# Six norms of a two-model kernel computed in two halves of the tokens, three decay levels merged into one, one exponential moved ahead of copies

## The chip, the cores and the metric

The kernel runs on one core of one Trainium2 chip. The metric is the device time of one execution in microseconds (us); the median of a few runs is compared with that of the kernel before. A profiled execution gives the trace that is read here.

## The reference, cut to what matters

Two transformer stacks run one after the other on a residual stream x of 256 tokens by 1,024 channels, all in fp32.

The first stack has two layers. Each takes h = rms_norm(x) * (1 + sc1) + sh1, multiplies it by `w_in`, runs three mixers on the parts (A: axial rotary attention; B: a gated linear recurrence in both directions of time; C: dilated local attention), and adds g1 * (mix @ `w_out`) to x. A second norm, a gated convolutional feed-forward (`w_up`, `w_down`) and a second addition follow. Mixer B needs attn[t, s] = sum over k of q[t,k] * key[s,k] * exp(b[t,k] - b[s,k]) for s <= t, b being the running sum of the logarithm of the forget gate, and the mirror of it backwards.

The second stack has a "fox" attention layer and an "NSA" attention layer, each followed by a norm and by experts (PEER): 8 heads choose 16 of 16,384 experts for each token. The factors sc, sh and g are 1,024-long dot products of a condition vector with the rows of "ada" matrices.

Every norm needs a mean over all channels of x, so it needs all output tiles of the product before it.

## The kernel before

**Layout.** Channels lie on the 128 partitions and tokens along the free dimension: `xT` and `hT` are [128, 8, 256]. A product is made tile by tile: `tile_T` (L748) takes one 128x1024 block of weights (a unit, 512 KB) from `ring`, a ring of eight, and accumulates eight fp32 matmuls of 256 columns into half of one PSUM bank. Each fp32 matmul is two MATMUL and two LDWEIGHTS instructions in the trace. Two tiles are a job in one of four banks (`open_job` L736, the plan L513 to L547).

**A norm** (`norm_stat` L741, `norm` of ScalarE L1183 and of VectorE L1651, `residual` L1659). There are eight, o = 0 to 7. VectorE adds job k of the product before into `xT` (L1666), ScalarE squares two channel tiles (L1188), TensorE sums all squares by eight matmuls with ones, ScalarE takes the root (L1190), VectorE the reciprocal (L1649), then scales the eight channel tiles (L1656), ScalarE shifts each (L1195), and the next product begins at the first shifted tile. Norms 1 and 3 stand between `w_out` and `w_up` of the two layers, 2 and 4 after `w_down`, 5 and 7 after the output products of the second stack and before the expert queries ("pq"); 0 is the first, and 6 stands between the experts and NSA.

**Decay levels** (mixer B; `level` L774, `decay` L1207, the loop L1802). The decay is not factored over a whole sequence but by halving blocks. Level k has blocks of 256 >> k tokens and takes the reference of b in the middle of each, so that no exponent is positive. VectorE forms the differences (L1808), ScalarE two pairs of exponentials (L1219), VectorE multiplies keys and queries with them (L1816, L1817), TensorE makes eight matmuls of 128 columns, and VectorE copies what is new under a mask (L1828). There are eight levels and a ninth without decay, the diagonal. Levels 0 to 5 stand between tiles of `w_in`; 6, 7 and the diagonal come after the last of them. Rotary steps of mixer A (L1790 to L1798) stand beside steps 6 and 7 on VectorE. Attention begins when all nine are copied (L867).

**Queues.** SP issues the units and the ada loads in an order written out by hand (L662 to L701). An ada load has one of four slots and waits for VectorE's dot product of four before (L645); `do_ada` (L1622) on VectorE waits for the load. In layer 0, 20 ada loads stand between units 27 and 28, and tiles 6 and 7 of `w_out` are made of units 28 and 29. In the fox layer two ada loads follow each unit from the eighth on (L701), 16 in all; VectorE makes their dot products (L2083) ahead of the forget-gate steps (L2089 to L2097), for which ScalarE waits (L1474) ahead of further copies.

**Experts** (L929, L1258, L1982). VectorE picks experts (`choose` L1906); the first choice's gates need ScalarE's exponential (L1328) of a difference that VectorE makes at L1934. ScalarE comes to it behind two copies of tokens (L1278) and six transfers that it issues itself (L1282). TensorE turns the first choice (`rows_of` L972) after the fourth expert unit of the first group.

## Time and profile before

| | us |
|---|---|
| median of 3 runs (2563.29 to 2564.15) | 2563.31 |
| profiled execution | 2559.09 |
| its span, first to last instruction | 2557.3 |
| TensorE matmul busy | 2438.8 |
| weight loads busy | 2276.6 |
| VectorE busy | 1630.7 |
| ScalarE busy | 849.5 |
| GpSimd busy | 282.0 |

The profiled execution lies 4.2 us under the median. Matmuls overlap, so TensorE's busy time is read as the time in which something was in the array. The mean granted TensorE clock is 0.983 of full speed. DMA moved 729 MB at 285 GB/s on average.

### The profile page before, as it was taken

Reading aid. Unit: us, or ns where it says so; the run is one execution under the profiler, and the core shown is the slowest. Engines: PE = TensorE matmul, PEld = TensorE weight load, DVE = VectorE, ACT = ScalarE, POOL = GpSimd, SP = SyncE. Lnnn points to the kernel's source line nnn. Section 1 sums busy time; section 2 is a strip of 40 time slices with the busy share of each in tenths; the row PEclk is TensorE's granted clock in tenths of the full one; section 3 lists DMA queues with packets and bytes.
Section 4 is the critical chain, followed back from the end, with each engine's and each line's share of the span. In section 5 each row is a group of like instructions: output and inputs, shape, how many; then the busy total and the mean of one; then the engine's idle time right before and its main releaser. Section 6 shows DMA issues by size and latency. Waiting matters only on the chain.

```text
span 2557.3 us, 44536 instructions
## 1 busy us (share of the span) xinstructions
PE 2438.8 (95%) x16628; PEld 2276.6 (89%) x16628; DVE 1630.7 (64%) x3720; ACT 849.5 (33%) x2165; POOL 282.0 (11%) x374
## 2 busy tenths in 40 slices
PE   5978999989999999999999999999999999999999
PEld 4867888878888888899999999988888999999999
DVE  6685664575565562497788884333637958888733
ACT  2541110254211022222665551012532246655300
POOL 0020110001011001011111111100210101111111
PEclk8999999999999999999999999999999999999999
DMA  9327887521687873399999999964026999999997
GB/s 365 117 81 262 302 308 286 198 84 43 246 305 271 312 266 98 114 370 414 342 403 385 404 406 412 397 243 164 18 83 227 404 355 401 408 379 410 408 414 297
DMA packets 172059, 729.13 MB, mean 285 GB/s; under 512 B 19216, under 2 KB 19728, under 8 KB 146960
## 3 DMA queue, kind: packets, MB, share of 16 engines
q1 hardware_dynamic: 143568, 523.92, 55.2%
q0 software_dynamic: 27648, 201.34, 19.4%
q10 hardware_dynamic: 704, 2.10, 0.3%
q8 instruction: 77, 1.26, 0.2%
q14 instruction: 62, 0.51, 0.1%
HBM read 724.14 MB, written 1.05 MB: 284 GB/s over the span
## 4 chain that ended last, share of the span: by engine, by line
PE 87%; DVE 5%; DMA 3%; ACT 3%; issue 2%; ACTq 0%; SPq 0%; DVEq 0%
PE banks L721 39%; PE lev L1019 22%; PE banks L965 20%; PE lev L721 2%; DMA extra<-in_ada 1%; DMA ring<-in_peer_u 1%; PE lev L946 1%; PE banks L946 1%; ACT arena L1219 1%; DVE arena L1632 1%; DVE arena L1776 1%; DVE rstd L1649 1%; ACT arena L1245 1%; DMA arena<-in_ada 0%; PE lev L818 0%
## 5 line engine op out<-in xcount | busy, mean ns | idle before, releaser
L721 PE MATMUL banks<-hT,ring 128*128 128x256 f32 x2832 | 631.3, 386 | 41.8 <-ACT hT L1195 40.9
L721 PEld LDWEIGHTS banks<-hT,ring 128*128 128x128 f32 x2832 | 547.6, 194 | 124.0 <-issue 45.3
L965 PE MATMUL banks<-hT,ring 128*128 128x160 f32 x4096 | 578.8, 301 | 2.3 <-DMA ring<-in_peer_u 2.3
L1019 PE MATMUL lev<-arena,ring 128*128 x4096 | 576.5, 301 | 0.0
L965 PEld LDWEIGHTS banks<-hT,ring 128*128 128x128 f32 x4096 | 559.2, 190 | 3.4 <-DMA ring<-in_peer_u 2.0
L1019 PEld LDWEIGHTS lev<-arena,ring 128*128 128x128 f32 x4096 | 558.9, 190 | 0.0
L1603 POOL DMA_INDIRECT arena<-in_peer_rows,keysb x192 | 184.2, 959 | 1147.7 <-DVE consts L1992 671.3
L721 PE MATMUL banks<-arena,ring 128*128 128x256 f32 (+1 forms) x1344 | 280.6, 371 | 6.0 <-DMA ring<-in_stream_first 4.6
L721 PEld LDWEIGHTS banks<-arena,ring 128*128 128x128 f32 x1344 | 246.4, 191 | 38.7 <-issue 5.0
L2039 DVE SCALAR_TENSOR_TENSOR extra<-consts,chT 128x192 bf16<-128x192 f32 x640 | 223.7, 409 | 26.5 <-ACT arena L1286 26.4
L2004 DVE CUSTOM_DVE_ANT_0 arena<-arena 128x1024 f32<-128x1024 f32 x64 | 78.2, 1222 | 166.0 <-DMA arena<-in_peer_rows,keysb 166.0
L1632 DVE CUSTOM_DVE_ANT_0 arena<-arena 128x1024 f32<-128x1024 f32 x104 | 127.6, 1227 | 58.8 <-DMA arena<-in_ada 55.4
L1992 DVE SCALAR_TENSOR_TENSOR consts<-arena,extra,consts 128x1024 f32<-128x1024 f32 x128 | 164.0, 1281 | 0.0
L2004 DVE CUSTOM_DVE_ANT_0 arena<-arena,consts 128x1024 f32<-128x1024 f32 x128 | 155.5, 1215 | 0.3
L1286 ACT ACTIVATE arena<-banks 128x320 f32<-128x320 f32 x128 | 55.8, 437 | 275.1 <-PE banks L965 256.8
L1580 POOL TENSOR_SCALAR arena<-arena,rinv 128x256 f32<-128x256 f32 (+1 forms) x128 | 63.4, 508 | 729.0 <-DVE rinv L1703 557.6
L1311 ACT ACTIVATE std<-consts,chT 128x128 bf16<-128x128 f32 x320 | 102.1, 390 | 82.7 <-PE banks L946 65.9
L1632 DVE CUSTOM_DVE_ANT_0 arena<-extra,arena 128x1024 f32<-128x1024 f32 x88 | 109.2, 1240 | 31.6 <-DMA extra<-in_ada 28.2
L1311 ACT ACTIVATE rstd<-consts,chT 128x128 bf16<-128x128 f32 x320 | 102.0, 390 | 73.3 <-PE banks L946 54.6
L1436 ACT ACTIVATE arena<-banks,params 128x256 f32<-128x256 f32 x88 | 44.9, 561 | 244.6 <-PE banks L721 244.6
L1300 ACT ACTIVATE extra<-extra 128x1 f32<-128x1 f32 x192 | 37.3, 194 | 265.5 <-DVE extra L2004 265.5
L721 PE MATMUL lev<-arena 128*128 128x128 f32 (+1 forms) x544 | 101.6, 331 | 23.3 <-DVE arena L1817 16.1
(275 smaller groups left out, 2254.3 us busy)
## 6 DMA issues: line engine op xcount, KB each, us to landing
ring<-in_peer_u SPq DMA_DIRECT2D x256, 512.0 KB
ring<-in_peer_v SPq DMA_DIRECT2D x256, 512.0 KB
ring<-in_stream_first SPq DMA_DIRECT2D x192, 512.0 KB
arena<-in_ada SPq DMA_DIRECT2D x104, 512.0 KB, 5.2
extra<-in_ada SPq DMA_DIRECT2D x88, 512.0 KB, 5.3
ring<-in_stream_nsa SPq DMA_DIRECT2D x45, 512.0 KB
ring<-in_stream_fox SPq DMA_DIRECT2D x41, 512.0 KB
arena<-in_peer_rows,keysb POOLq DMA_INDIRECT x192
```

What stands on the lines that cost most here:

```text
L721: ins = nc.tensor.matmul(o, lhsT, rhs, start=start, stop=stop, **kw)
L946: ins = nc.tensor.matmul(gate_banks[half][k % 2][:, t * 256:t * 256 + HALF], hot_r[:, k % 2, t], hot_c[:, k % 2, t, i], start=i == 0, stop ...
L965: ins = nc.tensor.matmul(banks[k // 2 % 4][:, (k % 2) * ND:(k % 2 + 1) * ND], ring[:, u % RING, c], hT[:, c, NS:T], start=c == 0, stop=c = ...
L1019: ins = nc.tensor.matmul(lev[c // 4][:, (c % 4) * T + NS:(c % 4 + 1) * T], ring[:, u % RING, c], a[:, bass.ds(g, 1), k], start=False, stop ...
L1286: A(acts_g[:, g, 2 * k:2 * k + 2], banks[k][:, 0:2 * ND].rearrange("p (a t) -> p a t", a=2), ACT.Gelu_apprx_tanh).then_inc(sem("act_freed" ...
L1311: A(dist[q % 2][:, t], iota, ACT.Abs, bias=chT[:, 0, 4 * q + t:4 * q + t + 1])\
L1580: G.tensor_scalar(x, x, rinv[:, u % 4, hh:hh + 1], 1.0, ALU.mult, ALU.mult).then_inc(sem("probs_ready"), 1)
L1603: G.indirect_dma_start(out=rows[:, n % ROWS], out_offset=None, in_=io["peer_rows"], in_offset=bass.IndirectOffsetOnAxis(ap=eid[:, k:k + 1] ...
L1632: seq(V.tensor_tensor_reduce(out=junk, in0=ada_slot(n), in1=crow[:, l // DEPTH], scale=1.0, scalar=0.0, op0=ALU.mult, op1=ALU.add, accum_o ...
L1992: V.scalar_tensor_tensor(out=y, in0=rows[:, n % ROWS, D:2 * D], scalar=row_act[:, k:k + 1], in1=y, op0=ALU.mult, op1=ALU.add).then_inc(sem ...
L2004: V.tensor_tensor_reduce(out=u, in0=u, in1=xn[i], scale=1.0, scalar=0.0, op0=ALU.mult, op1=ALU.add, accum_out=row_act[:, k:k + 1]).then_in ...
L2039: ins = V.scalar_tensor_tensor(out=hot_c[:, q % 2, t], in0=iota[:, half * HALF:(half + 1) * HALF].unsqueeze(1).broadcast_to([P, PARTS, HALF]),
```

## The change

Three edits. (1) In norms 1, 2, 3, 4, 5 and 7, the last two output tiles are made for tokens 0 to 127 first and 128 to 255 after, each half in its own bank; the addition, the squares, the sum, the root, the reciprocal, the scaling and the shift are done by half, and the first two tiles of the next product too. The two units of such a pair are waited for together and released together. VectorE's ada turns are moved off the fourth job (`ADA_OUT` 4, 4, 3, 3 to 5, 5, 4, 0; turns of 6 to 8, 8, 8, 0), and `mods` stand before the addition of the first half. (2) Decay levels 5, 6 and 7 become one, with blocks of eight tokens and the reference in their middle; its exponents may be positive. Its product is made twice, from the 64 partitions of each direction of time, and copied under two masks; the diagonal comes before these two. (3) In the experts the first exponential stands ahead of ScalarE's token copies; the turning of the choices and ScalarE's part of it stand two units later.

```diff
+NDEC, NLEV = 6, 8
...
+    lv[:, 8], lv[:, 9] = np.where(fwd, 1, -1), np.where(fwd, -1, 1)
...
+    same = [(p[:, None] // b == p[None] // b) for b in (64, 32, 16, 8)]
+    lm = same[:3] + [np.eye(P), same[3] & (p[:, None] < p[None]), same[3] & (p[:, None] > p[None])]
...
+        def plan_halves(o):
+            for t in range(TT):
+                plan(("half", o), 1, t)
+                plan(("norm", o), 1, t)
...
             plan(("up", l), FC)
-            plan(("down", l), 4)
-        plan(("norm", 4), 1)
+            plan(("down", l), 3)
+            plan_halves(2 * l + 2)
...
-        ADA_TURNS = [[24] + [2] * FC + [6] * 4, [0] + [2] * FC + [6] * 4]
...
+        ADA_TURNS = [[24] + [2] * FC + [8, 8, 8, 0], [0] + [2] * FC + [8, 8, 8, 0]]
+        ADA_LEVELS, ADA_UNITS, ADA_OUT = [4, 0], [[0] * 6 + [1] * 6, [0] * NATT], [(5, 5, 4, 0), (0, 0, 0, 0)]
...
-                    state["pending"] = True
+                    state["pending"] -= 1
+
+            def next_unit(hold=False):
+
+                if hold:
+                    state["held"] += 1
+                elif state["unit"] >= 0:
+                    state["pending"] += 1 + state["held"]
+                    state["held"] = 0
                 state["unit"] += 1
...
+            def norm_part(o, t, chunks):
+
+                b = open_job("norm", o, t) if 0 in chunks else bank_of("norm", o, t)
+                for c in chunks:
+                    if t == 0 and c == 6:
+                        pe.wait_ge(sem("sq_half"), HALVED.index(o) + 1)
+                    elif c % 2 == 0:
+                        pe.wait_ge(sem("sq_ready"), 4 * o + c // 2 + 1)
+                    mm(b[:, 0:P], ones, sq[:, c, half_of(t)], c == 0, c == DC - 1,
+                       None if c < DC - 1 else filled("norm", o, t)[0])
+
...
+
+                w = [next_unit(), next_unit(hold=True)]
+                for t in range(TT):
+                    b = open_job("half", o, t)
+                    for k in range(2):
+                        for c in range(DC):
+                            mm(b[:, k * P:(k + 1) * P], w[k][:, c], src[:, c, half_of(t)], c == 0, c == DC - 1,
+                               filled("half", o, t)[0] if k and c == DC - 1 else None)
+                        if t and not k:
+                            norm_part(o, 0, (6, 7))
+                    norm_part(o, t, range(6))
+
+            def first_tiles(j, o):
...
+
+                n = HALVED.index(o)
+                b = open_job(*j)
+                w = [next_unit(), next_unit(hold=True)]
+                for t in range(TT):
+                    for k in range(2):
+                        for c in range(DC):
+                            if k == 0:
+                                pe.wait_ge(*((sem("h_ready"), DC * o + c + 1) if t else (sem("h_half"), DC * n + c + 1)))
+                            mm(b[:, k * T + t * P:k * T + (t + 1) * P], w[k][:, c], hT[:, c, half_of(t)], c == 0, c == DC - 1,
+                               filled(*j)[0] if t and k and c == DC - 1 else None)
+                        if t == 0 and k == 0:
+                            norm_part(o, 1, (6, 7))
 
...
                     pe.wait_ge(sem("lev_freed"), g - 1)
                 if l > 0 and k < 2:
...
-                qq = eq[:, k % 2] if k < 8 else qB
+                at = min(k, NDEC - 1)
+                if k != 5:
+                    pe.wait_ge(sem("keys_decayed"), l * NDEC + at + 1)
+                    pe.wait_ge(sem("queries_decayed"), l * NDEC + at + 1)
+                kk, qq = (fk, qB) if k == 5 else (ek[:, at % 2], eq[:, at % 2])
+                side = slice(0, HD) if k == 6 else slice(HD, P) if k == 7 else slice(0, P)
                 out_ = lev[g % 2][:, :].rearrange("p (h t q) -> p h t q", h=4, t=TT)
                 for h in range(4):
                     for t in range(TT):
...
                            signal=sem("lev_filled") if h == 3 and t == 1 else None)
...
                            signal=sem("lev_filled") if h == 3 and t == 1 else None)
 
...
+                for k in (6, 7):
                     level(l, k)
-                pe.wait_ge(sem("lev_freed"), 9 * (l + 1))
+                pe.wait_ge(sem("lev_freed"), NLEV * (l + 1))
...
-                for k in range(4):
...
-                norm_stat(2 * l + 1)
-                for k in range(FC):
+                last_tiles(2 * l + 1, mixT)
...
 
+                o = 2 * l + 2
+                halves = [open_job("half", o, t) for t in range(TT)]
+                for c in range(FC):
+                    at = 6 * FC + c
+                    if at % 8 == 0:
+                        w = next_unit()
+                    for t in range(TT):
+                        mm(halves[t][:, 0:P], w[:, at % 8], zT[:, c, half_of(t)], c == 0, c == FC - 1)
+                blocks = []
+                for t in range(TT):
+                    for c in range(FC):
+                        at = 7 * FC + c
+                        if t == 0:
+                            if at % 8 == 0:
+                                w = next_unit(hold=True)
+                            blocks.append(w[:, at % 8])
+                        mm(halves[t][:, P:2 * P], blocks[c], zT[:, c, half_of(t)], c == 0, c == FC - 1,
+                           filled("half", o, t)[0] if c == FC - 1 else None)
+                        if t and c == 7:
+                            norm_part(o, 0, (6, 7))
+                    norm_part(o, t, range(6))
...
-                inputs(NG // 2 - 1, NG // 2, False, {2: turn_choices})
+                inputs(NG // 2 - 1, NG // 2, False, {4: turn_choices})
...
+
...
+                n = HALVED.index(o)
+                for k in range(3):
+                    wait(sem("x_ready"), 4 * (o - 1) + k + 1)
+                    square(k, full, "sq_ready")
+                wait(*freed("half", o, 0))
+                square(3, half_of(0), "sq_half")
+                root(0, half_of(0))
+                for c in range(DC):
+                    wait(sem("half_scaled"), 8 * n + c + 1)
+                    shift(c, half_of(0), "h_half")
+                    if c == 1:
+                        wait(sem("x_ready"), 4 * (o - 1) + 4)
+                        square(3, half_of(1), "sq_ready")
+                root(1, half_of(1))
                 for c in range(DC):
...
             def drain(dst, *j):
...
+                    wait(sem("lev_filled"), l * NLEV + k - 1)
+                if k == NDEC - 1:
+                    for dst, c in ((eq, 8), (ek, 9)):
+                        A(dst[:, k % 2], dl[:, k % 2], ACT.Exp, scale=lvl[:, c:c + 1]).then_inc(sem("decays"), 2)
+                    return
                 d = dl[:, k % 2].rearrange("p h (n s m) -> p (h n) s m", s=2, m=m)
...
+
+                exp_of(0, 0)
                 wait(sem("xn_filled"), p + 1)
...
-                exp_of(0, 0)
...
                         choices()
                 for step in range(2 * GATES):
...
 
...
+                    add(bank_of("half", o, t), 3, half_of(t), P, freed("half", o, t))
+
+                def scale(t, c, signal):
...
-                        else:
-                            ins.then_inc(sem("x_half"), 1)
-                    wait(*freed(*name, k))
+                    add(bank_of(*name, k), k, slice(0, T), T, freed(*name, k))
                     dve.sem_inc(sem("x_ready"), 1)
+                do_ada(beside[3])
+                if late:
+                    late()
+                add_half(0)
+                wait(*freed("norm", o, 0))
+                seq(V.reciprocal(rstd[:, half_of(0)], std[:, half_of(0)]))
+                for c in range(DC):
+                    scale(0, c, "half_scaled")
+                    if c == 1:
+                        add_half(1)
+                        dve.sem_inc(sem("x_ready"), 1)
+                wait(*freed("norm", o, 1))
+                seq(V.reciprocal(rstd[:, half_of(1)], std[:, half_of(1)]))
+                for c in range(DC):
+                    scale(1, c, "h_scaled")
 
...
 
             def k_norms(dst, raw, rs, lo, hi):
...
```

## Rows read from the trace of the kernel before

**Rows 1.** the page, part 1 and the first two lines of part 5 for TensorE.
```profile
PE 2438.8 (95%) x16628; PEld 2276.6 (89%) x16628; DVE 1630.7 (64%) x3720; ACT 849.5 (33%) x2165; POOL 282.0 (11%) x374
...
L721 PE MATMUL banks<-hT,ring 128*128 128x256 f32 x2832 | 631.3, 386 | 41.8 <-ACT hT L1195 40.9
L721 PEld LDWEIGHTS banks<-hT,ring 128*128 128x128 f32 x2832 | 547.6, 194 | 124.0 <-issue 45.3
```

**Rows 2.** waits of TensorE: engine, line, waited for: us in total, times, longest.
```profile
PE banks L721 <- ACT hT L1195: 40.9, 8, 15.9
...
PE lev L721 <- DVE arena L1817: 16.1, 6, 4.4
...
PE banks L721 <- DMA ring<-in_stream_first: 4.6, 1, 4.6
PE lev L1044 <- DVE arena L1965: 4.6, 2, 2.7
```

**Rows 3.** timeline around norm 3: start, us, engine, line, operation, count [idle before <-releaser].
```profile
648.94 0.63 ACT L1188 ACTIVATE arena<-xT 128x512 f32<-128x512 f32 x1 [6.27 <-DVEq L1674]
651.42 0.47 ACT L1190 ACTIVATE std<-banks,epsc 128x256 f32<-128x256 f32 x1 [1.85 <-PE banks L721]
651.93 1.75 DVE L1649 RECIPROCAL rstd<-std 128x256 f32<-128x256 f32 x1 [3.08 <-ACT std L1190]
653.72 3.26 DVE L1656 SCALAR_TENSOR_TENSOR hT<-xT,gscale,rstd 128x256 f32<-128x256 f32 x8
654.24 3.31 ACT L1195 ACTIVATE hT<-hT,mod 128x256 f32<-128x256 f32 x8 [2.34 <-DVE hT L1656]
...
654.89 9.48 PE L721 MATMUL banks<-hT,ring 128*128 128x256 f32 x35 [3.51 <-ACT hT L1195]
```

**Rows 4.** stretches: A:B us, PE, PEld, DVE, ACT, POOL busy (count), PEclk, DMA.
```profile
652.74:656.15 3.41, 1.26 (x6) 1.16 (x7) 3.37 (x8) 1.91 (x5) 0.00 (x0) 1.00 0.00 0
656.15:659.56 3.41, 3.41 (x10) 2.66 (x9) 0.82 (x3) 1.39 (x4) 0.00 (x0) 0.50 0.48 154
567.40:581.06 13.66, 9.31 (x42) 9.07 (x43) 10.31 (x12) 1.92 (x3) 0.00 (x0) 0.50 0.00 1
```

**Rows 5.** chain that ended last: start, us, what.
```profile
83.10 6.91 PE banks L721 x32
...
102.20 7.16 PE banks L721 x64
...
209.33 6.66 DMA ring<-in_stream_first
...
920.54 6.29 DMA extra<-in_ada
```

**Rows 6.** ScalarE instructions of 128 columns, by form.
```profile
L1311 ACT ACTIVATE std<-consts,chT 128x128 bf16<-128x128 f32 x320 | 102.1, 390 | 82.7 <-PE banks L946 65.9 <-PE lev L946 16.3
```

**Rows 7.** timeline of TensorE, output tiles 6 and 7 of layer 0.
```profile
216.12 8.69 PE L721 MATMUL banks<-arena,ring 128*128 128x256 f32 x32 [4.63 <-DMA ring<-in_stream_first]
```

**Rows 8.** timeline of TensorE, statistics of fox queries and keys.
```profile
936.48 1.12 PE L721 MATMUL banks<-arena,consts 128*128 128x512 f32 x2 [2.00 <-ACT arena L1465]
```

**Rows 9.** timeline of layer 0 from the sixth level to the attention.
```profile
127.61 1.23 DVE L1816 TENSOR_TENSOR arena<-arena 128x1024 f32<-128x1024 f32 x1 [9.57 <-ACT arena L1219]
...
130.00 1.30 DVE L1828 COPY_PREDICATED arena<-arena,lev 128x1024 f32<-128x1024 uint32 x1
...
131.66 6.20 ACT L1219 ACTIVATE arena<-arena,consts 128x512 f32<-128x512 f32 x8
...
137.34 3.64 PE L721 MATMUL lev<-arena 128*128 128x128 f32 x16 [4.42 <-DVE arena L1817]
...
138.57 0.69 DVE L1790 TENSOR_TENSOR arena<-banks,consts 128x512 f32<-128x512 f32 x1
...
150.92 1.99 PE L721 MATMUL lev<-arena 128*128 128x256 f32 x8 [1.45 <-DVE arena L1828]
```

**Rows 10.** timeline of the first experts' choice: token copies, exponential, TensorE's wait.
```profile
1085.10 3.48 ACTq L1282 DMA_DIRECT2D arena<-extra  x4
...
1090.26 0.22 DVE L1959 TENSOR_REDUCE gsum<-arena 128x4 f32<-128x64 f32 x1 [6.08 <-ACT arena L1292]
...
1093.31 0.61 PE L1044 MATMUL lev<-arena,consts 128*64 128x96 f32 x12 [1.87 <-DVE arena L1965]
```

More of the change, by code:

```diff
@@ L525, in build @@
         plan(("attF",), 8)
-        plan(("foxout",), 4)
-        plan(("norm", 5), 1)
+        plan(("foxout",), 3)
+        plan_halves(5)
         for k in range(4):
@@ L717, in _ @@
         def _(pe):
-            state = {"unit": -1, "pending": False}
+            state = {"unit": -1, "pending": 0, "held": 0}
             def mm(o, lhsT, rhs, start=True, stop=True, signal=None, **kw):
@@ L1069, in _ @@
             mixed[0] = [(sem("conv_out"), 1)]
-            for k in range(4):
+            for k in range(3):
                 b = open_job("foxout", k)
@@ L1165, in _ @@
             mixed = {c: [freed("attN", 2 * c + t) for t in range(TT)] for c in range(8)}
-            for k in range(4):
+            for k in range(3):
                 b = open_job("nsaout", k)
@@ L1192, in norm, with square, root @@
-                l, w = o // 2, o % 2
+                l, w = o // 2, o % 2
+                def square(k, of, signal):
+                    A(sq[:, 2 * k:2 * k + 2, of], xT[:, 2 * k:2 * k + 2, of], ACT.Square).then_inc(sem(signal), 1)
+                def root(t, of):
+                    wait(*filled("norm", o, t))
+                    b = bank_of("norm", o, t)
+                    A(std[:, of], b[:, 0:of.stop - of.start], ACT.Sqrt, bias=epsc[:, :], scale=1.0 / D)\
+                        .then_inc(freed("norm", o, t)[0], 1)
@@ new lines, in shift @@
+                def shift(c, of, signal):
+                    A(hT[:, c, of], hT[:, c, of], ACT.Identity, bias=mod[:, l, 3 * w, c:c + 1]).then_inc(sem(signal), 1)
+                full = slice(0, T)
+                if o not in HALVED:
+                    for k in range(4):
+                        if o:
+                            wait(sem("x_ready"), 4 * (o - 1) + k + 1)
+                        square(k, full, "sq_ready")
+                    root(0, full)
+                    for c in range(DC):
+                        wait(sem("h_scaled"), 8 * o + c + 1)
+                        shift(c, full, "h_ready")
+                    return
@@ new lines, in norm @@
+                n = HALVED.index(o)
+                for k in range(3):
+                    wait(sem("x_ready"), 4 * (o - 1) + k + 1)
+                    square(k, full, "sq_ready")
+                wait(*freed("half", o, 0))
[7 more added lines that the diff above has]
+                        square(3, half_of(1), "sq_ready")
@@ L1657, in norm, with residual, add, add_half @@
                                            op0=ALU.mult, op1=ALU.mult).then_inc(sem("h_scaled"), 1)
-            def residual(name, l, which, beside=(0, 0, 0, 0)):
-                for k in range(4):
+            def residual(o, name, l, which, beside=(0, 0, 0, 0), late=None):
+                def add(b, k, of, w, signal):
+                    for j in range(2):
+                        c = 2 * k + j
+                        V.scalar_tensor_tensor(out=xT[:, c, of], in0=b[:, j * w:(j + 1) * w],
+                                               scalar=mod[:, l, which, c:c + 1], in1=xT[:, c, of],
+                                               op0=ALU.mult, op1=ALU.add).then_inc(signal[0] if j else sem("x_half"), 1)
+                    wait(*signal)
+                def add_half(t):
+                    wait(*filled("half", o, t))
+                    add(bank_of("half", o, t), 3, half_of(t), P, freed("half", o, t))
+                def scale(t, c, signal):
+                    V.scalar_tensor_tensor(out=hT[:, c, half_of(t)], in0=xT[:, c, half_of(t)],
+                                           scalar=gscale[:, o // 2, o % 2, c:c + 1], in1=rstd[:, half_of(t)],
+                                           op0=ALU.mult, op1=ALU.mult).then_inc(sem(signal), 1)
+                for k in range(3):
```

135 lines of the change are left out of this document (56 added, 79 removed).

## The prediction

> **What bounds the kernel.** The engine line of the page comes first: TensorE is busy for 2438.8 us of 2557.3 [rows 1], so the kernel is a stream of matmuls with some 118 us of gaps, and a change is worth what it takes out of the gaps, less what it adds to the stream. The waits of TensorE say where the gaps are [rows 2]. For the first shifted tile of a norm: 40.9 us in eight waits, 15.9 of them at the kernel's start, so 3.57 for each of the other seven. For the decay levels: 16.1 in six. For the first expert choice: 4.6 in two. For a unit of weights: once, 4.6. The timeline of one norm shows a gap as a chain [rows 3]: root 0.47, reciprocal 1.75, one scaling, one shift, hand-overs; 3.51 idle. The stretches add its second price [rows 4]: with TensorE idle for most of 652.74 to 656.15, the next 3.41 us are granted half the clock (1.2 instead of 2.4 GHz), which costs half of them, 1.7. The other norm gaps are followed by the same, and in the levels of layer 1 the half clock lasts 13.66 us.
>
> **Narrow matmuls.** 64 of 128 columns take 7.16, 32 of 256 take 6.91 [rows 5]: 0.112 against 0.216, so two halves cost 0.008 more than a whole. Norms 1, 3, 5 and 7 turn 80 wide instructions into 160 (+0.64 each), 2 and 4 with their 22-deep products 136 into 272 (+1.1): 4.7 us in all. The Trainium skill (TensorE: Matmul & The Clock Gate, Back-to-back issue gap) speaks against this: in a stream of weight loads and matmuls it gives 81 ns at 128 columns where a lone one has 56, since the load sets the pace too. By that the 1184 narrow instructions would cost an estimated 30 us instead of 4.7.
>
> **A norm in halves, on one clock.** Time 0 is where TensorE, done with the first half of the last pair, begins six of its eight sums (1.34). Slopes for narrow operations: ScalarE 0.39 for 128 columns [rows 6], spaced about 0.30, root 0.37; VectorE takes 1.23 for 1024 and 0.69 for 512 columns [rows 9], so 1.05 ns a column: a scaling 0.35, spaced 0.26; the reciprocal 0.95 (half of 1.75 and some fixed cost). Additions of half 0 end at 0.9, squares at 1.35. TensorE has 1.34 of sums and 1.79 of second-half tile before it needs them at 3.13: no wait. Last sums at 3.58, root at 4.15, reciprocal 5.20, first shifts at 6.0 and 6.3; TensorE has the other tile (1.79) and six sums (1.34) until 6.71: no wait for chunks 0 and 1. VectorE then adds half 1, so chunk 2 comes at 7.45 and the rest 0.30 apart against 0.22 for a tile: the tile ends at 9.16 instead of 8.50, stall 0.66. Last sums of half 1 at 9.61; one tile (1.79) covers a chain of 2.58, stall 0.79; its eight shifts are spaced 0.30, stall 0.51. Sum 1.96, in three parts with matmuls between them; none is near the 3.51 after which the clock fell, and I take no loss of clock. Against it stand 3.72 (gap, and the first matmul's start) and 1.68 of clock: gain 3.72 + 1.68 - 1.96 - 0.64 = 2.8. After `w_down` it is 2.4.
>
> **The norms one by one.** 3, 5 and 7: 8.4. 2: 2.4. 1: unit 28 lands 6.66 us after its issue, behind 20 ada loads [rows 5], and TensorE waits 4.63 for it [rows 7]. The pair now starts when unit 29 has landed too, an estimated 1.25 later (729 MB in 2557 us is 1.8 us a unit on average, and the queue is fuller here); turns 5, 5, 4 let SP issue unit 28 when it did before, since the tenth dot product is bound by its load. 2.8 less 1.0 is 1.8. 4: the fox layer has 16 ada loads behind unit releases, then dot products, the forget gate, ScalarE's copies, and TensorE waits 2.00 for these [rows 8]; the last load takes 6.29 [rows 5] in a chain of four such rounds. Its third load follows unit 8, and unit 8 follows the release of unit 0, now held until the first pair is done: from the same start about 0.5 to 1.2 later than now. TensorE arrives 2.5 earlier and waits that much more. No gain, -0.8, and with some 5 us idle a lost clock stretch, taken at 1.4: -2.2. Norms together: 10.4.
>
> **Levels.** Before, after the sixth level (ended 132.9) TensorE waits 4.42 and again for levels 6 and 7, and attention starts at 150.92 [rows 9]. After: the merged decay is two exponentials of 1024 columns, 1.9 us in place of four at 2.9, both before level 5's place, so multiplications (2 x 1.2) end at 129.0; copy of level 4 1.3, rotary 3 x 0.7, copy of the diagonal from 133.0 to 134.3, rotary and key halves 2.9, then two copies of 1.3 end at 139.9. TensorE makes the two products by 136.5 and waits 3.4. Attention at 140.0: 10.9 earlier. Removed are VectorE's two differences and four multiplications, one copy, eight exponentials (6.20 [rows 9]), one product. Layer 1 has the same waits and twice the half clock [rows 4]: 12.0. The idle 3.4 may still cost a stretch of clock at the start of attention, mostly hidden by VectorE's work there; 0.6 each. Levels: 21.7.
>
> **Exponential.** VectorE waits 6.08 for it, because ScalarE issues transfers of 0.6 to 1.1 us each first; then 3.0 us of VectorE work end at 1093.3, where TensorE has waited 1.87 [rows 10]; the other layer makes it 4.6 [rows 2]. Moved, it ends at 1083.1 (a table load of 1.28), the choice at 1087.2, 4 us before TensorE wants it. The copies start 0.3 later; their transfers are first used by VectorE's rows, 30 us on. Row fetches begin some 5 us earlier and share the DMA with units; TensorE waits little there and I take 0. The choices turned two units later leave ScalarE 9 us for 5 us of work. Gain 4.6.
>
> **Sum.** 10.4 + 21.7 + 4.6 = 36.7. The profiled execution's 2559.1 becomes 2522.4. It lies 4.2 under the median 2563.3, which becomes 2526.6, my forecast. Alone it has 2516 to 2537.
>
> **Rivals.** (a) The halves give nothing: the scaling and shift chain waits for its own hand-overs twice, stalls double to 4, and the clock falls in some. For: three stalls instead of one, ScalarE waits 2.34 for a first scaling even now. Against: each is covered by 1.8 to 3.1 of matmuls. 36.7 - 10.4: 2537, up to 2543 with a lost stretch in each. 0.14. (b) Attention starts with the levels but its own chain (a reciprocal of 1.75 ahead of each of the first steps, outputs of mixer B at half clock) returns 10 of the 21.7: 2537. Against: that chain starts with the last copy in both kernels. 0.08. (c) The moved exponential does not do what it says, because VectorE next waits for the chosen rows or fetches take the DMA: 2531. 0.04. (d) Narrow matmuls stand 25 ns further apart, as in the page's rule: 1184 of them, 2551. The row of 64 in 7.16 is against it. 0.02. (e) Slower: a narrow matmul with new weights takes as long as its weight load, 0.194 [rows 1]. 1184 x (0.194 - 0.108) = 102 in place of 4.7: 2623. It turns slower where the spacing passes 0.143. Against: the same 0.112. 0.03. More than forecast, below 2516: 0.02. The forecast has 0.67.
>
> The range reaches from 2514 (all bounds on the good side: norm 4 even, no lost clock in attention, and 2 us of waits for DMA gone) to 2543, the end of (a). What a measurement of this kernel can tell from no change is about 0.2%, 5 us. Only (e) is slower; the same needs (a), (b) and (c) together.
>
> **What would show it.** Right: waits for L1195's successor fall from 3.5 to under 2.1 us in all for each halved norm, with clock 1.00 after them; the stretch from the sixth level to attention falls from 18 to 7 us; no wait of `rows_of`; the wait for fox statistics grows from 2.0 to about 5; tiles 6 and 7 of layer 0 start about 1 us later than now. Wrong: halved-norm waits above 3 us, narrow matmuls spaced over 0.12, or attention that starts early and ends no earlier.

## The result and the profile after

The changed kernel takes 2523.18 us (median of 4 runs, 2521.95 to 2524.96) beside 2563.30 of the kernel before (4 runs, 2560.57 to 2564.15): ratio 0.9846, 95% interval 0.9829 to 0.9863, so 40.1 us faster, where 36.7 were forecast. Run again later it took 2523.76 beside 2561.10, ratio 0.985 (0.9836 to 0.9863). The profiled execution has a span of 2523.2 after 2557.3: 34.1 less. It was the slowest of its four, while the profiled one of before lay 4.2 under its median, so 6 us of the gain don't show in the two traces. How much of the time TensorE's clock takes differs from execution to execution, and that is the main lesson of this case.

The page of the changed kernel, parts 1 and 5, answers to [rows 1]:

```profile
PE 2434.6 (96%) x17188; PEld 2288.6 (91%) x17188; DVE 1624.6 (64%) x3772; ACT 848.0 (34%) x2205; POOL 281.4 (11%) x374
...
L732 PE MATMUL banks<-hT,ring 128*128 128x256 f32 (+1 forms) x3024 | 631.9, 370 | 22.6 <-ACT hT L1279 22.4
L732 PEld LDWEIGHTS banks<-hT,ring 128*128 128x128 f32 x3024 | 554.0, 192 | 97.5 <-issue 21.7
```

TensorE issues 560 instructions more and is busy for 4.2 us less. It was busy at half clock for 64.0 us in the trace of before and for 40.0 in this one, which is worth 12.0 us of busy time; that outweighs what the narrow matmuls add. The other 29.9 of the 34.1 us are idle time that is gone. The waits of TensorE answer to [rows 2]:

```profile
PE banks L732 <- ACT hT L1279: 22.4, 8, 15.7
PE banks L732 <- ACT arena L1270: 18.7, 4, 14.7
...
PE lev L732 <- DVE arena L1968: 7.1, 2, 3.6
PE banks L732 <- issue: 4.2, 1, 4.2
PE banks L732 <- DVE arena L2223: 3.0, 1, 3.0
PE banks L1047 <- DMA ring<-in_peer_u: 3.0, 7, 0.8
PE banks L732 <- ACT arena L1581: 2.0, 1, 2.0
...
PE lev L732 <- DVE arena L1957: 1.2, 2, 0.6
```

One more line of the kernel before belongs beside these, the waits for copied levels:

```profile
PE lev L721 <- DVE arena L1828: 2.9, 2, 1.4
```

Waits for shifted tiles fell from 40.9 to 22.4, of which 15.7 is the start and 3.8 norm 6, still whole, which leaves 0.48 for each of the six halved norms. The levels cost 8.3 in four waits (7.1 for copies, L1968, and 1.2 for decayed queries, L1957), where before it was 19.0 in eight (2.9 for copies, L1828, and 16.1 for decayed queries, L1817). The wait at `rows_of` is gone. Two lines are new or larger: the statistics of fox (L2223 and L1581, 5.0 together, 2.00 and 0.88 before), and the small waits for units in the experts (3.0 in seven, 2.3 in three before).

Norm 3 in halves, in the timeline of the changed kernel (start, us, engine, line, operation, count [idle before <-releaser]), answers to [rows 3]:

```profile
620.37 1.95 PE L732 MATMUL banks<-arena,ring 128*128 128x128 f32 x16
...
622.80 0.37 ACT L1275 ACTIVATE std<-banks,epsc 128x128 f32<-128x128 f32 x1 [2.51 <-PE banks L732]
623.28 0.95 DVE L1804 RECIPROCAL rstd<-std 128x128 f32<-128x128 f32 x1 [3.44 <-ACT std L1275]
...
624.65 0.69 ACT L1279 ACTIVATE hT<-hT,mod 128x128 f32<-128x128 f32 x2 [1.48 <-DVE hT L1790]
...
625.73 2.62 PE L732 MATMUL banks<-hT,ring 128*128 128x128 f32 x16
...
630.60 2.45 ACT L1279 ACTIVATE hT<-hT,mod 128x128 f32<-128x128 f32 x8 [1.40 <-DVE hT L1790]
...
631.05 5.19 PE L732 MATMUL banks<-hT,ring 128*128 128x128 f32 x36 [0.48 <-ACT hT L1279]
```

And its stretches (A:B us, busy of PE, PEld, DVE, ACT, POOL with counts, PEclk, DMA share, GB/s), which answer to [rows 4]; the last four are the start of attention in the two layers:

```profile
631.05:635.21 4.16, 4.16 (x32) 4.16 (x33) 1.36 (x6) 2.00 (x7) 0.00 (x0) 1.00 0.44 174
635.21:642.10 6.89, 6.89 (x34) 6.09 (x33) 4.40 (x8) 1.02 (x2) 0.00 (x0) 1.00 0.75 271
137.55:140.96 3.41, 0.94 (x2) 0.84 (x3) 3.34 (x3) 0.00 (x0) 0.00 (x0) 0.50 0.00 0
140.96:144.38 3.42, 3.42 (x11) 2.81 (x10) 2.94 (x3) 1.02 (x4) 0.00 (x0) 0.50 0.02 5
553.97:557.39 3.42, 1.09 (x3) 0.92 (x4) 3.35 (x3) 0.00 (x0) 0.00 (x0) 0.50 0.00 0
557.39:560.80 3.41, 3.41 (x12) 2.87 (x11) 2.94 (x3) 1.02 (x4) 0.00 (x0) 0.50 0.00 0
```

Three small stalls stand where one of 3.51 was: sixteen instructions take 2.62 with shifts in step against 1.95 without (0.67), then 0.48 idle, then 32 in 4.16 where 32 at 0.112 take 3.57 (0.59). Together 1.74, and the clock is 1.00 behind them.

**Where the 34.1 us of the two traces come from.** The same point of the stream is looked up in both traces (start of a group of matmuls on the timeline), and the lead of the changed kernel is the difference.

| point | before | after | lead | gained since |
|---|---|---|---|---|
| w_out of layer 0 | 193.09 | 183.84 | 9.25 | levels 9.25 |
| second pair of w_up, layer 0 | 240.50 | 227.57 | 12.93 | norm 1: 3.68 |
| first level of layer 1 | 512.53 | 497.40 | 15.13 | norm 2: 2.20 |
| w_out of layer 1 | 622.63 | 597.23 | 25.40 | levels 10.27 |
| second pair of w_up, layer 1 | 663.56 | 635.21 | 28.35 | norm 3: 2.95 |
| second pair of fox | 900.38 | 871.68 | 28.70 | norm 4: 0.35 |
| first gap of fox attention | 988.53 | 964.29 | 24.24 | fox statistics: -4.46 |
| token copies' transposes | 1081.70 | 1054.51 | 27.19 | norm 5: 2.95 |
| second half of the experts | 1385.08 | 1355.44 | 29.64 | exponential: 2.45 |
| NSA attention, last gap | 1868.99 | 1838.32 | 30.67 | 1.03, clock behind norm 6 |
| transposes of the last experts | 1945.24 | 1911.62 | 33.62 | norm 7: 2.95 |
| second half of the last experts | 2248.41 | 2214.28 | 34.13 | exponential: 0.51 |

These are one execution of each kernel. Where the other traces tell more, the text below gives their numbers.

### The profile page after: what moved, and what is told of

Read it like the earlier page. It is cut to its first block, busy times and chain, and to the rows that moved or that the text cites. A ratio compares the mean times of both kernels' runs of the same rounds, so it can differ in the third digit from the quotient of the medians.

```text
span 2523.2 us, 45753 instructions
## 1 busy us (share of the span) xinstructions
PE 2434.6 (96%) x17188; PEld 2288.6 (91%) x17188; DVE 1624.6 (64%) x3772; ACT 848.0 (34%) x2205; POOL 281.4 (11%) x374
## 4 chain that ended last, share of the span: by engine, by line
PE 84%; DMA 7%; DVE 5%; ACT 2%; issue 2%; SPq 0%; DVEq 0%; ACTq 0%
PE banks L732 36%; PE lev L1101 22%; PE banks L1047 20%; DMA ring<-in_peer_u 3%; DMA extra<-in_ada 3%; PE lev L732 2%; DMA arena<-in_ada 1%; DVE arena L1748 1%; PE lev L1028 1%; PE banks L1028 1%; ACT arena L1361 0%; ACT arena L1335 0%; PE lev L873 0%; DVE arena L1832 0%; DVE arena L1968 0%
## 5 line engine op out<-in xcount | busy, mean ns | idle before, releaser
L732 PE MATMUL banks<-hT,ring 128*128 128x256 f32 (+1 forms) x3024 | 631.9, 370 | 22.6 <-ACT hT L1279 22.4
L732 PEld LDWEIGHTS banks<-hT,ring 128*128 128x128 f32 x3024 | 554.0, 192 | 97.5 <-issue 21.7
L732 PE MATMUL banks<-arena,ring 128*128 128x256 f32 (+2 forms) x1648 | 284.7, 334 | 5.5 <-issue 4.2
L732 PEld LDWEIGHTS banks<-arena,ring 128*128 128x128 f32 x1648 | 258.7, 192 | 30.3 <-issue 4.6
L1748 DVE CUSTOM_DVE_ANT_0 arena<-extra,arena 128x1024 f32<-128x1024 f32 x88 | 109.2, 1241 | 22.4 <-DMA extra<-in_ada 19.6
L1995 DVE SCALAR_TENSOR_TENSOR arena<-banks,params,arena 128x255 f32<-128x255 f32 x88 | 42.5, 483 | 107.4 <-ACT arena L1552 105.8
```

Source lines behind the costliest of these rows:

```text
L732: ins = nc.tensor.matmul(o, lhsT, rhs, start=start, stop=stop, **kw)
L1748: seq(V.tensor_tensor_reduce(out=junk, in0=ada_slot(n), in1=crow[:, l // DEPTH], scale=1.0, scalar=0.0, op0=ALU.mult, op1=ALU.add, accum_o ...
```

## The experiments

Twelve runs, each timed beside the kernel before. The times of before, in three groups of runs, were 2564.91, 2561.10 and 2561.82 (medians), so ratios are compared across groups. Each interval is about 0.0014 (3.6 us) to either side.

### The parts alone

Merged levels alone: on the kernel before, every hunk of the diff that has `NDEC`, `NLEV`, the masks or `decay` in it.

```
+NDEC, NLEV = 6, 8
...
-                for k in (6, 7, 8):
+                for k in (6, 7):
                     level(l, k)
```

> The kernel before with the merged decay levels alone. By the prediction's sum: 21.7 us off, so 2563.3 becomes 2541.6. By the marks of the two traces (start of attention, and the last attention gap, in each layer) it gives 9.25 in layer 0 and 10.25 in layer 1, 19.5, so 2543.8: 1.65 of each layer's gain is lost again in the first 3.4 us of attention, which run at half clock. Rival (b), that attention's own chain returns ten: 2552.

Measured: 2542.83, ratio 0.992 (0.9906 to 0.9934), 22.1 us between medians. The prediction's 21.7 stands; rival (b) falls.

The exponential alone, on the kernel before:

```
+                exp_of(0, 0)
                 wait(sem("xn_filled"), p + 1)
...
-                exp_of(0, 0)
                 done = 0
...
-                    if n == 28:
+                    if n == 29:
...
-                inputs(NG // 2 - 1, NG // 2, False, {2: turn_choices})
+                inputs(NG // 2 - 1, NG // 2, False, {4: turn_choices})
```

> The kernel before with the early exponential and the choices turned two units later alone. By the prediction: 4.6 us off (1.87 and 2.69 of waits at the first choice), 2558.7. By the traces, part of it comes back later in the experts as waits for units of weights, because the fetched rows start earlier and share the DMA: 3.1 off, 2560.2, with waits for units of more than 2 us in the profile. Rival (c), nothing comes of it: 2563.

Measured: 2556.24 (8 runs), ratio 0.9972 (0.996 to 0.9984): 8.7 us between medians, and 4.1 to 10.3 by the interval of the ratio, which still holds the prediction's 4.6 but not the 3.1. Rival (c), that nothing comes of it, falls.

Levels and exponential, both edits together, norms whole:

> The changed kernel with all norms whole: levels and exponential only. If the parts add, it stands 10.4 us above the changed kernel by the prediction, 10.6 by the marks of the traces: 2533.8 beside 2523.2. If halving gives nothing (rival a), it stands at the changed kernel's time, 2523. If halving interacts with the rest, it stands elsewhere than the sum of its parts run alone.

Measured: 2540.81, ratio 0.9915 (0.9899 to 0.993). The changed kernel stands 17.0 us lower (2523.76 in the next group), by the ratios 0.0065 or 16.7. The two intervals together leave 11 to 22 us for this difference. Trace against trace it is 12.9 and 13.7. Rival (a) falls, and halving is worth more than the 10.4 of the prediction, by how much is not certain.

### What a whole norm costs

The kernel of levels and exponential with the gap of each of the six norms filled by work that nothing reads:

```
 def norm_stat(o):
...
+    if o in (1, 2, 3, 4, 5, 7):
+        b = open_job("fill", o, 0)
+        for c in range(DC):
+            mm(b[:, 0:T], ones, cos, c == 0, c == DC - 1,
+               filled("fill", o, 0)[0] if c == DC - 2 else freed("fill", o, 0)[0] if c == DC - 1 else None)
```

> Levels and exponential only, all norms whole (as run third, 2540.8), with sixteen instructions of 128x256 on constants, 3.45 us, in the gap of each of the six norms that the change halves. It tells the two parts of a whole norm's price apart. Theory: the gap stays (now filled), and the half clock behind it goes; over five profiles with whole norms TensorE was busy at half clock for 22.7 us on average behind the six gaps, half of which is lost, so 11 us off, 2529 to 2530, and halving was worth 6 us of gaps besides. If the stretches of half clock do not come from the gaps: 2541.

Measured: 2527.81, ratio 0.9871 (0.9854 to 0.9888): 13.0 us under the kernel with whole norms (0.0044, 11.3, by the ratios), though no chain is shorter and TensorE runs 96 instructions more. The timeline of norm 1, first without and then with the filling:

```profile
214.60 3.62 PE L724 MATMUL banks<-arena,consts 128*128 128x256 f32 x16
221.79 8.51 PE L724 MATMUL banks<-hT,ring 128*128 128x256 f32 x25 [3.57 <-ACT hT L1199]
```

```profile
214.84 3.62 PE L730 MATMUL banks<-arena,consts 128*128 128x256 f32 x16
218.29 3.62 PE L730 MATMUL banks<-consts 128*128 128x256 f32 x16
222.03 3.26 PE L730 MATMUL banks<-hT,ring 128*128 128x256 f32 x14
```

Without it, the sum and the first tile lie 3.57 apart, and 25 instructions take 8.51. With it, the tile starts no sooner, and 14 take 3.26, the full rate. The stretches behind them, without and with:

```profile
220.80:224.21 3.41, 2.42 (x6) 2.00 (x7) 3.08 (x8) 3.07 (x8) 0.00 (x0) 0.50 0.04 7
224.20:227.60 3.40, 3.40 (x10) 2.68 (x9) 0.00 (x0) 0.24 (x1) 0.00 (x0) 0.50 0.42 152
```

```profile
222.00:226.00 4.00, 3.97 (x19) 3.53 (x20) 2.11 (x6) 2.68 (x7) 0.00 (x0) 1.00 0.41 135
```

So most of what halving won was the half clock behind the gaps, 11 to 13 us for six. What is left between this kernel and the changed one, 4 us by medians and 5 by the ratios, is what the gaps themselves won, less what fox gives back. Norm 3 shows both parts without mixture, from the start of `w_out` to the second pair of `w_up`, layer 1: 40.93 us in the three traces in which one stretch of half clock followed its whole gap, 39.24 in the one in which none did and also in the one with the gap filled, and 37.98 to 38.01 in all nine traces in which it is halved. Of these 2.9 us, 1.69 are clock and 1.25 are gap. The first of these two views also shows what the prediction missed: here the half clock lasts twice as long as in [rows 4]. In the traces of before and of the first three experiments (levels, exponential, both) there are 24 such gaps of 3.50 to 3.58 us, and one more in the next experiment. Behind 15 of the 25 came one stretch of half clock (3.41 us), behind 7 two (6.83), behind 3 none. TensorE was busy for 90.8 us of the stretches behind the 24, so a gap lost 1.9 us of clock on average. One of those with none, norm 4 of the kernel of the next experiment; the gap is the first stretch, from 859.74:

```profile
859.80:863.30 3.50, 0.00 (x0) 0.01 (x1) 2.91 (x4) 1.09 (x3) 0.00 (x0) 1.00 0.64 261
863.30:866.70 3.40, 3.38 (x16) 3.01 (x17) 3.12 (x11) 2.68 (x7) 0.00 (x0) 1.00 0.46 151
```

The profiled run of before had one stretch behind every one of its six. The price of a gap differs from execution to execution, and a single trace shows one draw of it. The runs bear it out: the twelve of the kernel before in the first group had mean clocks of 0.979 to 0.983 and spans from 2567.1 to 2556.7, correlated at -0.84. The Trainium skill (TensorE: Matmul & The Clock Gate, Part 1) also calls the number of slow matmuls run-variable, for those of a kernel's start. The traces here show the same behind gaps.

### Norm 4 and fox

Norm 4 whole again, its ada turns 6, 6, 6, 6, the rest as changed:

```
-        HALVED = (1, 2, 3, 4, 5, 7)
+        HALVED = (1, 2, 3, 5, 7)
...
-        ADA_TURNS = [[24] + [2] * FC + [8, 8, 8, 0], [0] + [2] * FC + [8, 8, 8, 0]]
+        ADA_TURNS = [[24] + [2] * FC + [8, 8, 8, 0], [0] + [2] * FC + [6, 6, 6, 6]]
...
-            first_tiles(("fin", FOX_ORDER[0]), 4)
+            norm_stat(4)
```

> The changed kernel with norm 4 (w_down of layer 1 to the fox projections) whole again and its ada turns 6, 6, 6, 6; the other five stay halved. By the traces, halving norm 4 lost 4.1 us: 2.1 in a wait of its sums for squares that wait for eight dot products, and 4.5 in the statistics of fox, against 2.5 won; so this one is 4.1 faster than the changed kernel, 2519.1. By the prediction (a loss of 2.2) 2521.0. If the late fox statistics only show what any earlier arrival meets, it is no faster.

Measured: 2521.53, ratio 0.9837 (0.9822 to 0.9852) against 0.985: 2.2 us less by medians, in different groups; the intervals overlap. It agrees with the prediction's loss of 2.2 and is too small to be certain. In its trace the waits at the fox statistics are 0.49, 2.00 and 0.87, near the 2.00 and 0.88 of the kernel before and not the 2.99 and 2.00 of the changed one, so the longer waits came with the halving of norm 4. The changed kernel again, for the comparisons that follow:

> The changed kernel again, on the chip of the next three, to compare them with. 2523 to 2525. In its profile the six halved norms leave gaps of 0.48 with clock 1.00 after them, and the experts have small waits for units. If the granted clock after a gap is a matter of where its window falls, its mean clock stays near 0.988 (five runs of levels and exponential alone had 0.983, twelve of the kernel before 0.981).

Measured: 2523.76, ratio 0.985. Its trace corrects one reading of the first. There, norm 4's sums had waited 2.13 us for squares behind ada dot products that waited for loads; here they run without a gap. Norm 4 in the first and in the second execution:

```profile
851.97 1.06 PE L732 MATMUL banks<-arena,consts 128*128 128x128 f32 x8
855.16 0.71 PE L732 MATMUL banks<-arena,consts 128*128 128x128 f32 x4 [2.13 <-ACT arena L1270]
```

```profile
852.57 1.50 PE L732 MATMUL banks<-arena,consts 128*128 128x128 f32 x12
```

What stays in both is the late start of the fox statistics, in the second execution 3.32 and 1.04:

```profile
906.17 2.08 PE L732 MATMUL banks<-arena,consts 128*128 128x512 f32 x2 [3.32 <-DVE arena L2223]
909.29 2.08 PE L732 MATMUL banks<-arena,consts 128*128 128x512 f32 x2 [1.04 <-ACT arena L1581]
```

Eight of the sixteen ada turns of the fox layer moved beside `w_out` of layer 1, otherwise as changed:

```
-        ADA_TURNS = [[24] + [2] * FC + [8, 8, 8, 0], [0] + [2] * FC + [8, 8, 8, 0]]
-        ADA_LEVELS, ADA_UNITS, ADA_OUT = [4, 0], [[0] * 6 + [1] * 6, [0] * NATT], [(5, 5, 4, 0), (0, 0, 0, 0)]
+        ADA_TURNS = [[24] + [2] * FC + [8, 8, 8, 0], [8] + [2] * FC + [8, 8, 8, 0]]
+        ADA_LEVELS, ADA_UNITS, ADA_OUT = [4, 0], [[0] * 6 + [1] * 6, [0] * NATT], [(5, 5, 4, 0), (4, 4, 0, 0)]
```

> The changed kernel with eight ada turns taken from the fox layer (16 to 8) and put beside w_out of layer 1 (4 and 4). Theory: fox statistics are late because of the loads and dot products ahead of them; then the two waits of 2.99 and 2.00 at 904.65 and 908.76 and the half clock behind them go, 4 to 6 us off, 2518; the wait of 2.13 in norm 4 stays. Against it: the eight loads stand ahead of units of w_out, which may cost a wait such as layer 0 has (4.18): then 2522. Rival: fox statistics wait for ScalarE's copies and VectorE's other work whatever the loads: 2523 or above.

Measured: 2515.05 (2513.38 to 2515.60), ratio 0.9815 (0.9802 to 0.9828): 8.7 us under the changed kernel, on the same chip, more than expected. The chain in the changed kernel's second execution, VectorE's last loads, dot products and what follows them:

```profile
899.79 1.23 DVE L1748 CUSTOM_DVE_ANT_0 arena<-extra,arena 128x1024 f32<-128x1024 f32 x1 [1.89 <-DMA extra<-in_ada]
...
903.84 1.76 DVE L2218 MEMSET arena<- 128x2048 f32 x1 [0.49 <-DVE gscale L1761]
905.64 0.47 DVE L2223 TENSOR_SCALAR arena<-banks,params 8x256 f32<-8x256 f32 x1
```

With eight fewer, VectorE waits for TensorE instead, and the eight statistics run in one piece:

```profile
888.98 1.76 DVE L2218 MEMSET arena<- 128x2048 f32 x1 [0.49 <-DVE gscale L1761]
...
894.86 0.47 DVE L2223 TENSOR_SCALAR arena<-banks,params 8x256 f32<-8x256 f32 x1 [4.12 <-PE banks L732]
...
901.50 3.60 PE L732 MATMUL banks<-arena,consts 128*128 128x512 f32 x8
```

In this pair of traces that is 4.36 of waits gone, and a half clock of 10.2 us from 905.49 on, in which TensorE had been busy for 8.5, which costs another 4.3: 8.6. In the first execution of the changed kernel the same two were 4.99 and 2.5. The eight loads cost `w_out` of layer 1 no wait.

### The gap ahead of attention

As changed, with sixteen instructions on constants after the last level:

```
                 for k in (6, 7):
                     level(l, k)
+                b = open_job("fill", l, 0)
+                for c in range(DC):
+                    mm(b[:, 0:T], ones, cos, c == 0, c == DC - 1,
+                       filled("fill", l, 0)[0] if c == DC - 2 else freed("fill", l, 0)[0] if c == DC - 1 else None)
```

> The changed kernel with sixteen instructions of 128x256 (products of constants that nothing reads, in a bank of their own, 3.45 us) in the gap of 3.55 between the last level and attention, in both layers. Theory: the half clock in attention follows from TensorE's idleness in that gap; filled, the stretches of half clock at 137.55 and 553.97 (busy for 4.35 and 4.51 in them) are gone and attention runs about 2.2 us shorter in each layer: 4.4 off, 2519. Rival: the stretch comes from the whole stage of levels, or attention's start is bound by VectorE's copies anyway: same time, 2523, or a little above.

Measured: 2520.37 (2518.91 to 2521.18), ratio 0.9836 (0.9823 to 0.985); the ranges of five runs each don't overlap. 3.4 us less: the half clock there did follow from the gap. The timeline of TensorE in layer 0:

```profile
136.41 3.72 PE L733 MATMUL banks<-consts 128*128 128x256 f32 x16
140.07 1.99 PE L733 MATMUL lev<-arena 128*128 128x256 f32 x8
```

The clock in the stretch that follows, which was 0.50 without the filling:

```profile
140.00:143.41 3.41, 3.41 (x23) 3.14 (x23) 3.31 (x4) 0.85 (x4) 0.00 (x0) 1.00 0.02 5
```

Attention starts at 140.07, as in the changed kernel, and eight instructions take 1.99 at once. Half a microsecond per layer is given back at its next wait for ScalarE (1.06 instead of 0.59).

### The wait ahead of norm 1

As changed, with the twenty ada loads beside `w_out` issued in two lots:

```
                     if k == U_IN + 5:
-                        load_ada(ADA_TURNS[l][0] - ADA_LEVELS[l])
+                        load_ada(min(10, beside_out))
+                    if k == U_IN + 7:
+                        load_ada(max(0, beside_out - 10))
```

> The changed kernel, with the twenty ada loads beside w_out of layer 0 issued in two lots of ten and the next two units of weights between them. Theory: TensorE's wait of 4.2 to 4.5 ahead of the halved pair of norm 1 is SP's queue, which issues unit 28 only behind the twentieth load (at 199.1, although its place in the ring had been free since before attention); then the gap and the half clock behind it go, 5 to 7 us off, 2517 to 2519. Rival: the pair then waits for the dot products (five, five and four beside w_out) that delay the additions: about 2522.

Measured: 2517.19, ratio 0.9824 (0.981 to 0.9837), beside 0.985 of the changed kernel one group earlier: 6.6 us less by medians. SP's queue in the changed kernel (second execution) and in this one:

```profile
170.13 3.12 SPq L660 DMA_DIRECT2D arena<-in_ada  x2
185.22 1.59 SPq L660 DMA_DIRECT2D extra<-in_ada  x2
...
199.10 3.64 SPq L666 DMA_DIRECT2D ring<-in_stream_first  x7
```

```profile
168.92 3.12 SPq L660 DMA_DIRECT2D arena<-in_ada  x2
172.08 8.02 SPq L666 DMA_DIRECT2D ring<-in_stream_first  x2
```

SP stood still from 173 to 185 behind a load whose slot waited for a dot product of VectorE (12.0 us). Let past it, the next unit is issued at once, at 172.08, and the one after it at 179.8, when TensorE releases its place in the ring (7.2 us of waiting), and the wait of 4.36 is gone altogether. From the start of `w_out` to the second pair of `w_up` this trace has 38.7 us, where the seven traces with a halved norm 1 and the old order have 43.7 to 45.8.

### The exponential and the choices

As changed, with the edit of the exponential alone (above) undone: the exponential behind the copies, the choices at the old place.

> The changed kernel with the first exponential behind the token copies and the choices turned at the old place. By the prediction it is 4.6 slower, 2527.8; by the profile's marks 3.1, 2526.3, since waits for units (1.1 in the first experts, 2.2 in the second) go when the wait of 1.87 and 2.69 for the choice comes back. Alone on the kernel before it was worth 8.7 between medians, on top of the levels 2.0.

Measured: 2531.13 (4 runs), ratio 0.9876 (0.9861 to 0.9891): 7.4 us slower than the changed kernel. The waits of TensorE, and the stretches behind the first of the two:

```profile
PE lev L1126 <- DVE arena L2099: 5.7, 2, 2.9
```

```profile
1065.37:1068.79 3.42, 2.73 (x19) 2.39 (x20) 3.35 (x21) 0.00 (x0) 0.00 (x0) 0.50 0.92 205
1068.79:1072.20 3.41, 3.41 (x15) 3.41 (x14) 3.34 (x25) 0.00 (x0) 0.77 (x1) 0.50 0.50 175
```

The waits are 5.7, and behind the first of them 6.14 us of matmuls ran at half clock: 3.1 more. The kernel before had the same two waits at 1.87 [rows 10] and 2.69 and no half clock behind either.

All traces together give a better price than any pair. From the first matmuls of the token copies to the second half of the experts, both expert layers added, the three traces with the late exponential (before, levels alone, and this one) take 606.6 to 610.1 us, mean 608.9, and the eleven with the early one 601.2 to 604.3, mean 602.9. That is 6.0 us, with no overlap.

The second part of this edit, undone alone (`{2: turn_choices}` and `n == 28`):

> The changed kernel with the choices turned two units earlier, at the old place. By the prediction ScalarE has 9 us for 5 us of work at either place, so no difference: 2523.8. If the later turning is needed (the copies of the choices would wait), a wait of TensorE of 1 to 4 us comes in each of the two expert layers: up to 2531. If the later turning costs, it is faster.

Measured: 2523.48, ratio 0.9849 (0.9836 to 0.9863). No difference, as the prediction said.

### A version that beats both

Two lots, eight turns earlier and the filled gap, together:

> All three together: ada loads in two lots, eight turns earlier, filled gap ahead of attention. If they add: 2523.8 - 6 - 8.7 - 3.4 = 2505.7. If some share one cause, up to 2512.

Measured: 2504.64 (2503.00 to 2508.51), ratio 0.9777 (0.9762 to 0.9791): 57.2 us under the kernel before and 19.1 under the changed one, where the three alone gave 8.7, 6.6 and 3.4, which is 18.7. They add, within the intervals. In its trace no gap of TensorE over 1.9 us is left but those of the kernel's start and of norm 6, the one norm that was not halved (3.57).

## Why the prediction was right, and where its terms were off

**Narrow matmuls: right.** The price of 0.008 a pair came from the stream itself. In the changed kernel 132 narrow ones of `w_down` start from 837.24 to 851.86, 0.112 apart, half of the 0.216 of wide ones. Rivals (d) and (e) fall. The Trainium skill (TensorE: Matmul & The Clock Gate, Back-to-back issue gap) has 81 ns at 128 columns in such a stream where a lone matmul has 56. That surcharge does not show in these fp32 instructions.

**A norm in halves: the chain right, the clock's price too low.** Stalls were put at 0.66, 0.79 and 0.51 and are 0.67, 0.48 and 0.59. The marks give 2.95 each for norms 3, 7 and 5 where 2.8 was said, and 2.20 where 2.4 was. But "the next 3.41 us are granted half the clock, which costs half of them, 1.7" took one execution's stretch for the price. TensorE was busy at half clock behind the six gaps for 20.1 us in the trace of before, for 25.1, 24.1 and 21.5 in the next three, and filling the gaps gave 11 to 13 us where 1.68 times six is 10.1. By the average of the four traces the clock term is short by 1.3 us, and norm 1 adds about 0.5. Why halving brought some 17 and not 10.4 is not shown beyond these: the rest is 5 us, as much as the interval of that 17 to either side.

**Norm 1: right on average, 3.68 in the two traces by luck.** From the start of `w_out` to the second pair of `w_up` in layer 0, the four traces with a whole norm 1 take 45.98 to 49.35 us, mean 47.4, and the seven with a halved one and the old order of loads 43.73 to 45.81, mean 45.1: 2.3 us, near the 1.8. The profiled execution of the changed kernel is the shortest of the seven. "An estimated 1.25 later" for the second unit holds too. The tiles of unit 28 start 5.8 to 6.8 us after its issue where one unit is waited for, and 7.1 to 8.1 where two are, means 6.4 and 7.5, although SP issues unit 29 only 0.4 us behind unit 28. The sign "tiles 6 and 7 of layer 0 start about 1 us later" failed in this pair of traces: counted from the start of `w_out` they start 0.45 sooner, since unit 28 was issued 0.78 sooner. Over all traces with merged levels they start 0.6 later.

**Norm 4: right in its mechanism, its size open.** "TensorE arrives 2.5 earlier and waits that much more" with a lost stretch gave -2.2. The wait is 5.0 and 4.4 in the two executions, "about 5" in the prediction. The lost clock was larger than the 1.4 taken: TensorE was busy at half clock for 5.0 us in one and 8.5 in the other, which costs 2.5 and 4.3, and that is also why moving eight loads brought 8.7. The marks have norm 4 at -4.1 with the fox statistics, the medians of the kernel with norm 4 whole at -2.2 with intervals that overlap.

**Levels: right.** Attention at 140.02 was forecast at 140.0. Forecast 21.7, alone 22.1 by medians and 20.5 by the ratio. By the marks it is 19.5, because the lost clock at the start of attention, taken at 0.6 a layer as "mostly hidden", came to 1.65; filled, it gave 3.4 back in two layers, so it was not hidden.

**Exponential: right in its mechanism, short in its size.** The waits went (4.6 in the trace of before), and "I take 0" for the earlier row fetches was nearly so: waits for units are 3.0 and 2.7 in the two executions, 2.3 before. In the two traces it brought 3.0; over all fourteen it is 6.0, where 4.6 was forecast. What the trace of before did not show is lost clock behind the same waits, which other executions have: 6.14 us busy at half in the trace with the late exponential, 6.43 in that of the levels alone. The medians, 8.7 alone, 7.4 undone in the changed kernel and 2.0 on top of the levels, scatter around the 6.0 by about their intervals.

That 2526.6 came within 3.4 us of 2523.18 is in part luck. The sum was made on an execution 4.2 under its median, the one of the four traces with whole norms in which the clock lost least behind them. The forecast added the same 4.2 to the changed kernel, although fewer gaps are left there for the clock to fall behind. The medians have 40.1 us where 36.7 were forecast, the traces 34.1: the mechanisms were right, and the clock's price was taken from a single draw.

## What to carry to other kernels

A gap of TensorE of 3.5 us cost itself and, in most executions, 1.5 to 3.1 us of clock behind it, 1.9 on average over 24 gaps. For a gap that a split can only shrink, this second part was the larger gain (1.69 of the 2.9 us of norm 3). It differs from run to run, so price it from several executions and judge by medians, or measure the same piece of the stream in every trace there is. It can be taken away by splitting the work so that only gaps of half a microsecond are left, or, without touching the chain, by matmuls on constants in a bank of their own. When a queue is ordered by hand, look for what stands behind a blocked entry although its own buffer is free: two units let past ten loads were worth 6.6 us here.

## What had not been expected of the hardware

The same 3.5 us of idleness was followed by no half clock, by 3.41 us or by 6.83 us of it, in one and the same kernel. Smaller gaps are no safer in kind: behind the 2.00 us ahead of the fox statistics (with a wait of 0.5 to 0.9 closely behind it) none followed in the trace of before, and 6.83, 6.83 and 3.41 us in the next three; in one trace 6.83 us followed a gap of 2.75 and none one of 2.93. And a stream of matmuls whose results nothing reads makes the kernel 11 to 13 us faster, with 96 instructions more.

Half clock also came with no gap at all. In NSA attention 64 matmuls of 15 columns stand in a row. In all fourteen traces the clock fell to half 3.1 to 4.8 us after the first of them, for 10.24 us (13.65 in one), though TensorE had been without a gap for 12 us. In the changed kernel, the group on the timeline and the stretch that follows:

```profile
1757.83 9.60 PE L732 MATMUL banks<-arena 128*128 128x15 f32 x64
1762.29:1772.50 10.21, 10.21 (x49) 10.21 (x49) 9.10 (x21) 1.09 (x3) 0.00 (x0) 0.50 0.16 51
```

Half of that, 5.1 us, is lost in every kernel here, the fastest too. Whether it comes from the 15 columns was not tried.
